# A two-layer decoder trunk: norm sums and mean moved, conv work and weight units divided anew between the engines

## What is computed

```python
# layer 0
h = rms_norm(x, norm_g)
a, bv, bg, z = split(h @ w_in)             # 1024 | 1024 | 1024 | 2048
ya = grouped_linear(trailing_means(a) - a) * pool_scale
u  = causal_depthwise_conv(bv * sigmoid(bg), width=31) + conv_b
yb = silu(layer_norm(u, cn_g, cn_b))
x  = x + (concat(ya, yb) * silu(z)) @ w_out
# layer 1: rms_norm, q|k|v|z = h @ w_in, per-head norms, causal attention with ALiBi,
#          gate by silu(z), output projection, residual
```

## Time and profile before

| | |
|---|---|
| median of 3 runs | 341.54 us (341.4 to 341.61) |
| profiled execution | 341.72 us, of which span 339.9 us |
| TensorE (PE) busy | 330.2 us, 97% |
| VectorE (DVE) busy | 266.1 us, 78% |
| ScalarE (ACT) busy | 226.1 us, 67% |
| POOL busy | 37.6 us |

### The profile page before, as it was taken

How to read it: one execution, slowest core, us unless ns; L and a number is a source line. 1 busy time by engine, 2 the same in 40 slices (tenths; PEclk the granted TensorE clock), 3 DMA queues, 4 the chain that set the end, 5 groups by cost and what they waited for, 6 DMA issues and landing times.

```text
span 339.9 us, 5724 instructions
## 1 busy us (share of the span) xinstructions
PE 330.2 (97%) x2196; PEld 297.9 (88%) x2196; DVE 266.1 (78%) x493; ACT 226.1 (67%) x425; POOL 37.6 (11%) x50
## 2 busy tenths in 40 slices
PE   8999999999999999999989999999999999998995
PEld 8899999998989999989989999988887666787885
DVE  3998988999989999989787799648535776767433
ACT  5756776959799995149885457835757576675430
POOL 0000011223242201001100000004400211200000
PEclk9999999999999999999999999999999999999999
DMA  7987047898999858945959334691463333000003
GB/s 279 393 337 282 1 126 185 264 241 210 289 211 252 271 152 302 222 158 216 214 170 366 120 125 131 253 360 53 196 247 116 133 124 123 2 1 2 0 3 123
DMA packets 11691, 61.63 MB, mean 181 GB/s; under 512 B 1296, under 2 KB 1424, under 8 KB 5392
## 3 DMA queue, kind: packets, MB, share of 16 engines
q1 hardware_dynamic: 8064, 53.78, 43.8%
q0 software_dynamic: 3456, 7.34, 12.3%
q10 hardware_dynamic: 144, 0.15, 0.2%
HBM read 52.88 MB, written 1.05 MB: 159 GB/s over the span
## 4 chain that ended last, share of the span: by engine, by line
PE 55%; DVE 24%; ACT 11%; DMA 6%; issue 3%; SPq 0%; ACTq 0%; DVEq 0%
PE bank L997 14%; PE bank L999 14%; PE bank L998 14%; DVE w_lo L669 8%; DVE scratch L782 4%; PE bank L1031 4%; DVE scratch L787 4%; DMA w_lo<-raw 3%; DMA raw<-w 3%; ACT w_hi L409 3%; PE bank L1057 2%; PE bank L1215 2%; ACT scratch L492 2%; PE bank L1225 2%; ACT side_ring L467 1%
## 5 line engine op out<-in xcount | busy, mean ns | idle before, releaser
L669 DVE TENSOR_TENSOR w_lo<-raw,w_hi 128x1024 fp32r<-128x1024 f32 x76 | 89.2, 1219 | 10.6 <-ACT w_hi L409 10.3
L409 ACT CAST w_hi<-raw 128x1024 fp32r<-128x1024 f32 x80 | 79.3, 1045 | 5.6 <-PE bank L999 3.0
L997 PE MATMUL bank<-h_hi,w_hi 128*128 128x256 f32 x208 | 59.6, 287 | 0.6 <-DVE w_lo L669 0.6
L998 PE MATMUL bank<-h_lo,w_hi 128*128 128x256 f32 x208 | 58.9, 283 | 0.0
L999 PE MATMUL bank<-h_hi,w_lo 128*128 128x256 f32 x208 | 58.8, 283 | 0.0
L1031 PE MATMUL bank<-H,raw 128*128 128x256 f32 x256 | 56.8, 379 | 0.8 <-DMA raw<-w 0.8
L1031 PEld LDWEIGHTS bank<-H,raw 128*128 128x128 f32 x256 | 48.0, 190 | 7.2 <-DMA raw<-w 1.0
L782 DVE SCALAR_TENSOR_TENSOR scratch<-scratch,params 128x256 f32<-128x256 f32 x114 | 47.0, 477 | 4.4 <-ACT scratch L505 4.3
L997 PE MATMUL bank<-ya_hi,w_hi 128*128 128x256 f32 x160 | 47.3, 295 | 0.0
L998 PE MATMUL bank<-ya_lo,w_hi 128*128 128x256 f32 x160 | 45.2, 283 | 0.0
L999 PE MATMUL bank<-ya_hi,w_lo 128*128 128x256 f32 x160 | 45.2, 283 | 0.0
(11 more groups left out here) (101 smaller groups left out, 544.9 us busy)
## 6 DMA issues: line engine op xcount, KB each, us to landing
raw<-w SPq DMA_DIRECT2D x49, 1024.0 KB, 5.0
side_v<-side_ring POOLq DMA_DIRECT2D x20, 256.0 KB, 5.9
w_lo<-raw POOLq DMA_DIRECT2D x4, 512.0 KB, 7.7
X<-xT SPq DMA_DIRECT2D x2, 512.0 KB, 5.1
out<-X SPq DMA_DIRECT2D x4, 256.0 KB, 2.7
consts<-const SPq DMA_DIRECT2D x1, 290.0 KB, 13.4
params<-vec ACTq DMA_DIRECT2D x1, 149.0 KB, 4.8
```

What stands on the lines that cost most here:

```text
L409: nc.scalar.copy(halves(w_hi, cut_slot(n), half), halves(raw, n % RAW, half)).then_inc(hi_cut, 1)
L669: nc.vector.tensor_tensor(halves(w_lo, cut_slot(n), half), halves(raw, n % RAW, half), halves(w_hi, cut_slot(n), half).bitcast(F32), ALU.s ...
L997: nc.tensor.matmul(dst, wh, ah, start=start, stop=False, skip_group_check=True)
L998: nc.tensor.matmul(dst, wh, al, start=False, stop=False, skip_group_check=True)
```

## The change

- The sum of squares of layer 0 is taken by eight matmuls ahead of unit 0, without the fold, and there are 12 warm-up matmuls for 20. x times the gain goes to its own tile `H0` (the second half of SZ); only unit 0 uses it; unit 1 waits for the normed halves, and the unnormed halves are gone.
- The mean of the conv result: VectorE folds eight tiles to one (`fold_mean`, three adds), and one matmul sums it, within unit 22 (`MEAN_AT`: unit OA[1], second half, after output 4). The sum of squares goes from the middle of unit 23 to after output 3 of its second half (`SUM2_AT`).
- Native units before 22: 0, 5, 8, 11, 14, 17, 21 for 0, 5, 7, 9, 11, 13, 15, 17, 21. Unit 25 becomes native; unit 24 becomes an added unit in its place. Unit 22 uses slot 3 (`SPARE`), and the halves of yb wait for it.
- Side items 15 for 12. Products may also be given to slots 19 and 20, with a ring of two places in `side_v`, free once the side adds are done (`LATE_RING`). The planner favours the newest pair less early (`NEW_LAST`).
- Order: VectorE takes the gated value ahead of the cut of n+2; ScalarE does tap 0 ahead of the sigmoid.

Written out, the two planners' lists have 39 products and 114 single taps before; 44 and 92 after (in slots 17 to 21: 12 single; 6 single and two side adds; 4 products, 2 single; 6 products, 2 single and two side adds; 6 single).

```diff
-NATIVE = frozenset((0, 5, 7, 9, 11, 13, 15, 17, 21))
-ADDED = (22, 25)
-WARM = 20
+NATIVE = frozenset((0, 5, 8, 11, 14, 17, 21, 25))
+ADDED = (22, 24)
+SPARE = 22
+WARM = 12
...
-SIDE_ITEMS = 12
+SIDE_ITEMS = 15
 PRODUCTS = 4
+LATE_RING = 2
...
+def product_free(product):
+
+    if product >= LATE_FROM:
+        i = product - LATE_FROM
+        return FOLDED[i] if i < LATE_RING else PRODUCT_USED[product - LATE_RING]
+    return PRODUCT_USED[product - PRODUCTS] if product >= PRODUCTS else 0
...
-            if act_time > 0.8 and pair < (n - 1) // 2 and n <= LAST_PRODUCT:
+            if n == LAST_PRODUCT + 1 and late is None:
+                late = len(used)
+            if late is not None:
+                free = len(folded) >= LATE_RING or len(used) - late < len(folded)
+            else:
+                free = pair < (n - 1) // 2
+            if act_time > 0.8 and free and n < OA[0]:
...
+DVE_SHARE, ACT_SHARE, NEW_LAST = 0.95, 0.95, 40
+CONV_PLAN, TILE_DONE, PRODUCT_USED, LATE_FROM, FOLDED, HOMES = conv_plan()
+
+
+MEAN_AT = 1, 1, 4
+SUM2_AT = 2, 1, 3
+EARLY = (BG[0],), (Z1[0], Z1[1])
...
+        def product_home(product):
+
+            if product < LATE_FROM:
+                b = 2 * (product % PRODUCTS)
+                return PR[:, b:b + 2, :]
+            pair, chain = divmod(HOMES[(product - LATE_FROM) % LATE_RING], 2)
+            return side_v[:, pair, chain, :, :]
...
-            for m in range(4):
-                high_h(0, m)
-            cut_hi(1)
             take_root(bank[4], 1)
             prime(ACT.Sigmoid)
+            cut_hi(1, (0,))
+            high_h(0, 0)
+            high_h(0, 1)
+            cut_hi(1, (1,))
...
+                if n == OA[0]:
+                    cut_hi(OA[3])
                 if n == ZA[0]:
-                    act.wait_ge(tap, PRODUCT_USED[-1])
+                    act.wait_ge(tap, PRODUCT_USED[LATE_FROM - 1])
...
-            fold(0, 4)
-            for m in range(4):
-                low_h(0, m)
-            cut_lo(1)
             take_inverse(1)
+            normed_h(0, 0)
+            normed_h(0, 1)
+            cut_lo(1, (0,))
+            normed_h(0, 2)
+            low_h(0, 0)
+            low_h(0, 1)
+            normed_h(0, 3)
+            low_h(0, 2)
+            cut_lo(1, (1,))
+            low_h(0, 3)
             cut_lo(2)
...
+            def fold_mean():
+
+                for c in range(KD):
+                    dve.wait_ge(tap, TILE_DONE[c])
+                for i, n in enumerate((4, 2, 1)):
+                    if i:
+                        dve.wait_ge(mean_folded, i)
+                    src = SQ if i else V
+                    nc.vector.tensor_tensor(SQ[:, 0:n, :], src[:, 0:n, :], src[:, n:2 * n, :],
+                                            ALU.add).then_inc(mean_folded, 1)
...
+                    fold_mean()
+                    cut_lo(OA[2], (0,))
                     centre()
-                    cut_lo(n + 2)
+                    cut_lo(OA[2], (1,))
...
             for n in range(1, OA[0] + 1):
-                if n < OA[0]:
-                    cut_lo(n + 2)
...
                     nc.vector.tensor_tensor(U[:, 2 * i:2 * i + 2, PAD:PAD + S], value, SG2, ALU.mult).then_inc(u_ready, 1)
+                if n < OA[0]:
+                    cut_lo(n + 2)
...
+            square_sums(0, range(KD), bank[4], True)
             for n in range(PW):
...
             def channel_mean():
-                for c in range(KD):
-                    pe.wait_ge(tap, TILE_DONE[c])
-                    last = nc.tensor.matmul(bank[1][:, 0:S], ones[:, :], V[:, c, :], start=(c == 0), stop=(c == KD - 1),
-                                            skip_group_check=True)
-                last.then_inc(mean_sum, 1)
+                pe.wait_ge(sz_ready, 6)
+                pe.wait_ge(mean_folded, 3)
+                nc.tensor.matmul(bank[1][:, 0:S], ones[:, :], SQ[:, 0, :], start=True, stop=True,
+                                 skip_group_check=True).then_inc(mean_sum, 1)
...
-                    if i == 2 and kt == 0:
-                        square_sums(6, (0,), bank[2], True)
+                        if (i, kt, m) == MEAN_AT:
+                            channel_mean()
+                        if (i, kt, m) == SUM2_AT:
+                            square_sums(3, (0,), bank[2], True)
                 last.then_inc(unit_done, 1)
-
-                if i == 0:
-                    pe.wait_ge(sz_ready, 6)
-                    channel_mean()
```

More of the change, by code:

```diff
@@ L175, in conv_plan @@
 def conv_plan():
-    plan, last, used, count, before = {}, {}, [], 0, None
+    plan, last, used, count, before, late, folded, homes = {}, {}, [], 0, None, None, [], []
     left = {pair: [k for k in range(1, TAPS) if k not in side_taps(pair)] for pair in range(4)}
-    folds = list(range(2 * SIDE))
+    folds = [2 * pair + (SIDE_ITEMS + i) % 2 for pair in range(SIDE) for i in range(2)]
     dve_time = act_time = 0.0
@@ L204, in conv_plan @@
                 dve_time -= 0.8
-        while folds and n >= BG[folds[0] // 2 + 1] + SIDE_ITEMS + 1 + folds[0] % 2:
+        while folds and n >= BG[folds[0] // 2 + 1] + SIDE_ITEMS + (len(folds) + 1) % 2:
             tiles = CONV_PAIRS[folds[0] // 2]
@@ L274, in hybrid_trunk @@
         PR = SZ[:, 0:KD, :]
+        H0 = SZ[:, KD:2 * KD, :]
         SQ = YP
@@ L304, in hybrid_trunk @@
         minus_hi = sem("minus_hi")
-        lo_added = [sem(f"lo_added{i}") for i in range(2)]
+        lo_added = [[sem(f"lo_added{n}{half}") for half in range(2)] for n in ADDED]
         unit_done = sem("unit_done")
@@ L389, in _ @@
                     pool.dma_start(halves(w_lo, cut_slot(n), half).bitcast(F32), halves(raw, n % RAW, half),
-                                   accum_op=ALU.add).then_inc(lo_added[half], 16)
+                                   accum_op=ALU.add).then_inc(lo_added[i][half], 16)
             for r in range(8):
@@ L400, in _, with cut_hi @@
         def _(act):
-            def cut_hi(n):
+            def cut_hi(n, parts=(0, 1)):
                 if n >= NU or n in NATIVE:
@@ L407, in cut_hi @@
                     act.wait_ge(unit_done, slot_free(n))
-                for half in range(2):
+                for half in parts:
                     nc.scalar.copy(halves(w_hi, cut_slot(n), half), halves(raw, n % RAW, half)).then_inc(hi_cut, 1)
@@ L488, in _ @@
                         continue
-                    if product >= PRODUCTS:
-                        act.wait_ge(tap, PRODUCT_USED[product - PRODUCTS])
+                    if product_free(product):
+                        act.wait_ge(tap, product_free(product))
                     for i, c in enumerate(tiles):
-                        last = nc.scalar.mul(PR[:, 2 * (product % PRODUCTS) + i, :], U[:, c, k:k + S],
+                        last = nc.scalar.mul(product_home(product)[:, i, :], U[:, c, k:k + S],
                                              column(CW + TAPS * c + k))
                     last.then_inc(product_ready, 1)
+                if n in BG[1:] or n == A[0]:
+                    for c in (n - 2, n - 1):
+                        if c == n - 2:
+                            act.wait_ge(u_ready, n // 2)
+                        nc.scalar.activation(V[:, c, :], U[:, c, 0:S], ACT.Identity, bias=column(CB + c),
+                                             scale=column(CW + TAPS * c)).then_inc(first_tap, 1)
                 if n in BG:
@@ L1018, in channel_step @@
                     arrived(n, k // 4)
-                if h_wait == 0 and n in NATIVE:
+                if n == 0:
                     if k % 2 == 0:
@@ L1030, in channel_step @@
                     if n in NATIVE:
-                        last = nc.tensor.matmul(dst, wr, H[:, k, :], start=start, stop=stop, skip_group_check=True)
+                        last = nc.tensor.matmul(dst, wr, (H if n else H0)[:, k, :], start=start, stop=stop, skip_group_check=True)
                     else:
@@ L1070, in square_sums @@
                     pe.wait_ge(folded, folds)
-                else:
-                    pe.wait_ge(sq_ready, 12)
                 for c in tiles:
+                    if not folds and c % 2 == 0:
+                        pe.wait_ge(sq_ready, 8 + c // 2 + 1 if dst is bank[0] else c // 2 + 1)
                     summed = nc.tensor.matmul(dst[:, 0:S], ones[:, :], SQ[:, c, :], start=(c == 0),
@@ L1090, in _ @@
                 for k in range(KD):
-                    channel_step(n, k, {0: 0, 1: 0, 2: 1}.get(n))
-                    if n == 0 and k == 3:
-                        square_sums(3, (0,), bank[4], True)
+                    channel_step(n, k, 0 if n == 1 else None)
             n = PW
```

84 lines of the change are left out of this document (38 added, 46 removed).

## The result

The changed kernel takes **345.83 us** (median of four, 345.68 to 346.13), the kernel before 341.58 beside it (341.4 to 341.74): ratio 1.0126, 95% interval 1.0108 to 1.0143. It is 4.3 us slower. The forecast was 340.2, which is faster than before, with a range of 336.6 to 342.4; the time lies 3.4 us above its upper end.

What follows compares the result with a forecast made beforehand. TensorE's work was taken to bound the kernel, with VectorE nearest to being late. TensorE saves 5.9 us, waits at the mean and sum 2 give back 4.6: -1.35 from 341.54, so 340.2 us, range 336.6 to 342.4.

Steps and rivals of the forecast that it cites:

- TensorE's work: TensorE up to the start of unit 26: changed matmuls, stalls and formats together save about 5.9 us.
- Rival D: Start: clock not up by 7.1 us with fewer warm-ups, unit 0 2.9 us later, 343.1 us; chance 0.08.
- The stalls that were to go: TensorE's two stalls on early cuts (0.6 us) and unit 25's wait for the second added half (1.35 us) vanish.
- each cover that the forecast lists: Late units: normalising, low halves and SP's loads from unit 26 on come before they are due; nothing put for failures.
- VectorE's start: VectorE's first tap, at 32.04 us before, starts near 27.9 after work ahead of the taps is removed.
- VectorE's slots: Unit-by-unit lay-out of VectorE and ScalarE: slot 12 at 88.0, slot 18 at 125.2, fold at 153.3 before discount.
- The microsecond taken off: Discount on the lay-out, 2% too long for the old slots 12 to 18: folded mean ready at 152.3 us.
- The late products: Slots 19 and 20: ten products, ScalarE's 0.81 us each setting the pace for VectorE, which needs 0.6.
- rival C: Late products delay the fold: each microsecond past 152.3 costs one, slower by over 0.7 from 154.4; chance 0.14.
- its bound of 155 for the fold: Latest fold: ten late handovers each cost 0.2 us more and nothing is taken off; 342.9 us.
- Sum 2: Unit 23's second half: TensorE waits 2.1 us more for the sum of squares, after 2.5 at the mean.
- A's: The main forecast, 340.2 us, spanning 337.9 to 342.2 by the bounds of the fold; chance 0.48.

Runs made afterwards that it cites:

- experiment 2: Changed kernel without products in slots 19 and 20, whose ten pairs become single taps on VectorE: 342.24 us, ratio 1.0014.
- Experiment 6: Changed kernel with 36 extra unread matmuls ahead of the wait for the mean, so that TensorE stays busy: 344.83 us, ratio 1.0093.
- experiments 3: Changed kernel with ScalarE's cut of unit 22's high half a slot later, in slot 19: 344.85 us, ratio 1.0097.
- experiment 4: Changed kernel with 12 side items per pair for 15, and the planner's list made anew: 349.48 us, ratio 1.0226.
- 12: Changed kernel, eight native units, without late products, ScalarE's cut of unit 22 in slot 19, sum 2 after output 7: 342.15 us, ratio 1.0013.
- 13: Changed kernel with unit 15 native in the place of 17, the number kept at eight, list made anew: 343.80 us, ratio 1.0062.
- (8): Changed kernel with the weight units, side items and slots of before, leaving the start, the two sums and the new order: 343.46 us, ratio 1.0054.
- (9): Changed kernel with the old weight units, side items and slots, and both sums placed about half a unit earlier: 338.93 us, ratio 0.9914.

## Why the prediction was wrong, step by step

- **TensorE's work: right, a little too cautious.** -5.9 forecast at unit 26. Without the new waits the trace gives 0.8 less still: unit 1 began at 16.6 (17.0), unit 22 at 144.4 (145.15). The sums before unit 0 ran at the full clock from the first on: 16 instructions in 3.72 us, 0.216 apart; the forecast had the first two or three at 0.427. It put the clock's rise at 7.1 us; the warm-ups start 0.213 us apart up to 5.4 us and 0.11 from there, so it came before the sums. Rival D (clock not up) was wrong by the same rows.
- **The stalls that were to go: right.** Units 25's and the early cuts' waits are gone. Nothing behind unit 26 is new, and each cover that the forecast lists held. One that it doesn't list failed: the load of unit 22. Its list of SP's queue began at unit 26, and it never asked whether `raw` would be there when the spare unit's cut stands in slot 18, four units ahead.
- **VectorE's start: right.** First tap 27.9 forecast, 27.29 measured.
- **VectorE's slots: the step that failed.** The lay-out was within 0.4 us at slot 12 and 0.8 at slot 17 and then lost 3.5. It gave each operation its row's length but gave ScalarE no wait that wasn't VectorE's. The trace has two, 11.3 us together: 6.3 us for places in the ring of the side items, whose DMAs land after 7.1 us in the median (5.9 before), and 5.03 us for unit 22's load. VectorE's waits for ScalarE grew beside them: 2.73 at the cut of unit 19 (0.9 forecast), 2.54 at 13 (1.5), 0.95 at 16 (0.4), 0.92 at the gated pair. All its waits for high halves, over the whole span, are 17.2 us, 10.3 before. ScalarE was also not full from 80 to 120 us, as the forecast had it: 36.9 us busy of 40, and 37.8 before.
- **The microsecond taken off: wrong.** The same way of adding was 2% too long for the old slots and 6% too short for the new ones (slot 12 to the fold: 65.3 us by the lay-out, 69.2 in the trace). A stretch in which ScalarE waits 0.9 us for DMAs is no measure for one in which it waits 11.3.
- **The late products: mechanism right, size right.** The forecast had ScalarE set the pace; the trace has 0.86 for a pair and VectorE waiting 1.57, 0.25, 1.56, 0.24 and 0.25 us. Against single taps they cost 3.8 us (experiment 2), but most of that stood in the lay-out; beyond it slots 19 to 21 and the fold lost 0.8. So rival C had its slope right (a microsecond each past 152.3: at 157.6 that is 345.5, measured 345.83) and its place only in part: its bound of 155 for the fold came from handovers of late products alone, and the larger part arose in slots 17 and 18.
- **Sum 2: right in kind, not used.** 2.1 us forecast behind a wait of 2.5; after a wait of 8.65 there was none. Experiment 6 shows it again (1.2 us) as soon as the clock stays up.
- **The clock: not in the sum.** 2.1 us after the long wait. A forecast with a wait of 2.5 didn't need it; one whose range lets the fold come up to 5 us late did.
- **The range.** Its upper end rested on a fold at 155 at the latest; it came at 157.6. That bound let VectorE wait for ScalarE, but not ScalarE for DMAs, though one was seen to land only after 10.8 us. Nor did the range keep to its own bound: by the slope of rival C a fold at 155 gives 342.9, and the range ends at 342.4 (A's at 342.2).

The Trainium skill's rule in "VectorE: DVE Perf Modes", The DRAIN you can't avoid (a semaphore between chained operations costs nothing extra) would have had the fold ready sooner than the lay-out, and the trace has it later; the 2.4 us which the forecast estimated for it would have made the error larger.

What is shown: that the fold's time decides (experiments 2 to 4, 12 and 13, with the changed kernel six on one line); that one native unit more, with the list that the planner then makes, brings 5.6 us of it; that the late products cost 3.8; that unit 22's load goes with 1 to 2 (experiments 3 and 13, of which neither parts it from what moved with it). What stays open: how much of the rest is the ring of the side items, since no run took its wait away and left the work; and how much is the planner's list, since no run kept it and changed the native units.

## What to carry to other kernels

Where two engines hand work to each other and one of them also waits for DMAs, a microsecond of work that is moved onto them can cost more than one, and the main engine's gain is lost at the first point that needs the end of their chain: 1.15 us saved on TensorE put 2.6 us of work on VectorE, the fold came 5.6 us later, and the kernel lost 5.0. Lay out every queue on which such an engine can stand, DMA rings and in-order loads too, and take no discount from a stretch that hadn't these waits. Where a planner reads the constant that you change, compare its lists first. And when a sum or a hand-over is moved, ask who stands behind it on every engine: the same two matmuls half a unit earlier gained 4.5 us in one kernel, and half a unit later they lost 11 in another.

## What the runs showed of the hardware

- **After a long wait TensorE's clock is low.** The waits of 8.65, 4.7, 4.1, 3.7 and 3.4 us were followed by matmuls 0.21 us apart instead of 0.12 for some 3 to 6 us; those of 1.2 and 1.5 us weren't. In the changed kernel this cost 2.1 us, with TensorE kept busy nothing, but half of it came back as another wait.
- **At the start the clock rose while the warm-ups ran**, by the spacing at 5.4 us in the changed kernel and at 6.7 in the one before: instructions of 128 columns start 0.213 us apart ahead of it and 0.11 behind it. The 16 sums of 256 columns that follow 24 warm-ups ran 0.216 us apart from the first on (3.72 us). So the moment differs between two executions that begin with the same instructions.
- **The side adds took 5.9 to 8.1 us to land in the median, and their number didn't decide it.** The 256 KB side adds took 7.1 us from issue to landing in the median, 13.0 at most, for 5.9 and 9.7 before. That isn't shown to come from there being 26 for 20: with 20 of them the medians were also 7.7 (experiment 4), 8.1 (8) and 7.8 (9), and with 26 between 6.2 and 7.8.
